# Decoder layer on one core: the first three products of the up stage's first unit, run inside the mix stage

## The reference

```python
h = rmsnorm(x, norm_mix_pre);  proj = h @ w_in
pool_out = multiscale_pool(u_pool, w_pool)          # trailing means, 4 groups of 128
attn_out = stick_breaking_attention(q, k, v)        # 8 heads of 64
merged = concat(rms_normalize(pool_out) * pool_scale, rms_normalize(attn_out) * attn_scale)
mix = merged @ w_out                                # 1024 x 1024
x = x + rmsnorm(mix, norm_mix_post)
h = rmsnorm(x, norm_ffn_pre)
up = causal_depthwise_conv(h @ w_up, conv_w, conv_b)   # 1024 -> 2 x 2816, taps over 3 tokens
gate, val = up[..., :D_FF], up[..., D_FF:]
x = x + rmsnorm((silu(gate) * val) @ w_down, norm_ffn_post)
```

## Time and profile before

| | us |
|---|---|
| median of 3 runs | 2437.66 |
| lowest, highest | 2435.57, 2438.76 |
| the profiled execution's own time | 2436.97 |
| its span | 2435.3 |
| PE busy | 2331.2 (96% of the span) |
| DVE busy | 1817.9 (75%) |
| ACT busy | 1220.9 (50%) |
| POOL busy | 1026.2 (42%) |

### The profile page before, as it was taken

How to read it: one execution, slowest core, us unless ns; L and a number is a source line. 1 busy time by engine, 2 the same in 40 slices (tenths; PEclk the granted TensorE clock), 3 DMA queues, 4 the chain that set the end, 5 groups by cost and what they waited for, 6 DMA issues and landing times. The chain is left out here.

```text
span 2435.3 us, 36769 instructions
## 1 busy us (share of the span) xinstructions
PE 2331.2 (96%) x11673; PEld 1948.4 (80%) x11673; DVE 1817.9 (75%) x2137; ACT 1220.9 (50%) x2101; POOL 1026.2 (42%) x750
## 2 busy tenths in 40 slices
PE   8999999989999999996999999899999999999997
PEld 6787887878888888884888888688888878888876
DVE  5434224999999977878898899999999973344687
ACT  4311114889898975555444444544444433332444
POOL 0000002776666654656455554455455420122653
PEclk9999999999999999997999999999999999999999
DMA  6412347153333225676333233533333225445574
GB/s 192 145 42 89 128 135 193 32 147 92 85 92 87 81 82 173 211 243 214 103 113 103 90 108 102 204 96 108 103 112 103 90 106 174 170 168 203 200 254 160
DMA packets 264699, 324.71 MB, mean 133 GB/s; under 512 B 12996, under 2 KB 185980, under 8 KB 259580
## 3 DMA queue, kind: packets, MB, share of 16 engines
q1 hardware_dynamic: 262268, 314.72, 41.7%
q0 software_dynamic: 2304, 8.39, 0.9%
HBM read 213.48 MB, written 109.58 MB: 133 GB/s over the span
## 5 line engine op out<-in xcount | busy, mean ns | idle before, releaser
L810 POOL TENSOR_TENSOR weight<-beta,stick 128x512 f32<-128x512 f32 (+3 forms) x320 | 304.6, 960 | 539.7 <-ACT beta L749 422.2
L2151 DVE SCALAR_TENSOR_TENSOR x<-up_cols,taps,x 128x1024 f32<-128x1024 f32 x174 | 264.1, 1518 | 14.5 <-ACT x L2048 11.4
L861 DVE TENSOR_TENSOR_SCAN stick<-z_ps,stick,beta 128x512 f32<-128x512 f32 x192 | 245.0, 1276 | 13.2 <-ACT z_ps L750 12.0
L535 PE MATMUL out_ps<-hT,w_hi 128*128 128x512 f32 x768 | 239.6, 393 | 2.4 <-DVEq L462 2.4
L2138 DVE TENSOR_TENSOR wu_lo<-wu_sums,wu_hi 128x512 fp32r<-128x512 f32 x175 | 211.7, 1210 | 0.0
L749 ACT ACTIVATE beta<-z_ps 128x512 f32<-128x512 f32 (+3 forms) x320 | 171.4, 536 | 56.7 <-PE z_ps L893 49.8
L2035 ACT ACTIVATE wu_hi<-wu_sums 128x512 fp32r<-128x512 f32 x175 | 109.5, 627 | 164.0 <-PE gate_odd_ps L2281 90.7
L2281 PE MATMUL value_chain_ps<-wide,wu_hi 128*128 128x512 f32 x528 | 177.3, 390 | 1.9 <-DVE up_cols L2173 1.9
L910 PE MATMUL wT_ps<-ident,weight 128*128 128x128 f32 x1088 | 173.2, 275 | 3.1 <-POOL weight L810 3.1
L535 PEld LDWEIGHTS out_ps<-hT,w_hi 128*128 128x128 f32 x768 | 144.9, 189 | 34.6 <-DVEq L462 2.8
L750 ACT ACTIVATE z_ps<-z_ps 128x512 f32<-128x512 f32 (+3 forms) x320 | 172.2, 538 | 0.0
(11 more groups left out here) (272 smaller groups left out, 6184.7 us busy)
## 6 DMA issues: line engine op xcount, KB each, us to landing
wu_f<-in_w_up SPq DMA_DIRECT2D x44, 512.0 KB, 5.1
bridge<-in_w_up SPq DMA_DIRECT2D x44, 512.0 KB, 5.0
f_scratch<-f_sum SPq DMA_DIRECT2D x88, 256.0 KB, 2.0
down_lo<-f_scratch SPq DMA_DIRECT2D x44, 512.0 KB, 3.4
f_scratch<-x SPq DMA_DIRECT2D x66, 256.0 KB, 2.1
down_b<-in_w_down SPq DMA_DIRECT2D x65, 256.0 KB, 3.9
x_scratch<-x SPq DMA_DIRECT2D x56, 256.0 KB, 2.8
first_head<-qk_scratch SPq DMA_DIRECT2D x24, 512.0 KB, 9.8
```

Source lines behind the costliest of these rows:

```text
L535: m = pe.matmul(out_ps[half + j][:, :], w[slot][:, k, :], hT[h][:, k, j * BANK:(j + 1) * BANK], start=(k == 0 and t == 0), stop=(k == kc - ...
L810: pool.tensor_tensor(weight[v % weight_ring][:, 0:w], beta[v % stick_in][:, 0:w], stick[q % 2][:, at:at + w], ALU.mult).then_inc(weight_do ...
L861: dve.tensor_tensor_scan(stick[q % 2][:, at:at + w][:, ::-1], backwards, beta[u % stick_in][:, 0:w], start, ALU.mult, ALU.bypass).then_inc ...
L2151: dve.scalar_tensor_tensor(out=conv[h], in0=cols[:, h, 2 - back:2 - back + span], scalar=column(kind, h, e), in1=conv[h], op0=ALU.mult, op ...
```

## The change

Operands 0, 1 and 2 and the left operands a11, s1 and a12 are split within the steps of tiles 13 to 15 of mix, into tiles of their own. In PE's step 16, behind the last tile's attention product, stand three products of the up stage's unit 0: a11 with operand 0, s1 with operand 1, and (between the turn of tile 14 and the turn of tile 15) a12 with operand 2. ACT copies the first one's bank to `q` within mix. s2 and operands 3 and 4 (its high half) are also split or loaded at the end of mix. For this the weight block's load moves from step 12 to step 10, the loads of operands 0 and 1 from steps 13 and 14 to 11 and 12, operand 2's to step 15 ahead of the last product, operand 5's from up to the end of mix; POOL's `start_sums` moves from its end to the front of its step 12. SP no longer waits at the end of mix for the loads. The up stage begins with s2; DVE takes `keep_v`, operand 5 and `gate_part` first in unit 0. Scratch tiles change places so that the new ones fit.

```diff
@@ -1060,27 +1068,30 @@
                     if is_tile(t) and not (isinstance(t, int) and t < 2):
                         load_x(t, slot)
                     if isinstance(t, int) and t == tiles - 1:
+
+                        sp.wait_ge(mix_mm_done, done(t - 1))
+                        load_operand(2)
                         sp.wait_ge(mix_mm_done, done(t))
-                        for operand in range(2, 5):
-                            load_operand(operand)
+                        load_operand(3)
+                        load_operand(4)
                     if is_tile(t - 2):
                         store_x(t - 2, slot, uses - 1)
-                    if isinstance(t, int) and t == tiles - 4:
+                    if isinstance(t, int) and t == tiles:
+                        load_operand(5)
+                    if isinstance(t, int) and t == tiles - 6:
 
                         sp.wait_ge(even_out, stored(tiles // 4, 32))
                         sp.wait_ge(b22_out, stored(tiles // 4))
                         sp.wait_ge(sums_out, stored(tiles // 4, 64))
                         for h in range(2):
                             sp.dma_start(up_start["w_f"][:, h, :, :], w_up[0][:, h, :, :]).then_inc(start_w_in, 16)
-                    if isinstance(t, int) and tiles - 3 <= t < tiles - 1:
-                        load_operand(t - (tiles - 3))
+                    if isinstance(t, int) and tiles - 5 <= t < tiles - 3:
+                        load_operand(t - (tiles - 5))
 
                 def load_operand(operand):
-                    sp.dma_start(as_f32(up_start["x_lo"][operand]), s["x7"][operand][:, :, 0:BANK]).then_inc(start_x_in[operand], 16)
-
-                steps(sp, step, after_loop=4)
-                for operand in range(5):
-                    sp.wait_ge(start_x_in[operand], 16)
+                    sp.dma_start(as_f32(up_start["x_lo"][operand]), s["x7"][operand][:, :, 0:BANK]).then_inc(x7_in[operand], 16)
+
+                steps(sp, step, after_loop=6)
@@ -1103,6 +1114,8 @@
                     total(3, t4, b21, t2, ALU.subtract)
 
                 def step(t, slot, uses):
+                    if isinstance(t, int) and t == tiles - 4:
+                        start_sums()
                     if is_tile(t - 2) and slot == 1 and not (isinstance(t, int) and t == tiles + 1):
                         pool.wait_ge(copied, done(t - 2))
                         x_sums(uses - 1)
@@ -1130,8 +1143,7 @@
                     pool.tensor_tensor(s4, a12, s2, ALU.subtract).then_inc(start_sums_done, 1)
                     pool.tensor_tensor(s3, a11, a21, ALU.subtract).then_inc(start_sums_done, 1)
 
-                steps(pool, step)
-                start_sums()
+                steps(pool, step, after_loop=4)
@@ -1157,6 +1169,10 @@
                     act.activation(m_hi[slot][:, :, :], merged_of(t, slot), ACT.Copy).then_inc(m_hi_done, 1)
 
                 def step(t, slot, uses):
+                    if isinstance(t, int) and t == tiles - 1:
+                        act.wait_ge(m_lo_done, done(t))
+                        right_half(1)
+                        left_half(2, "a12")
...
@@ -1183,30 +1199,40 @@
                         else:
                             act.wait_ge(b22_out, stored(uses - 1))
...
+                    if isinstance(t, int) and t == tiles - 1:
+                        act.wait_ge(m_sum, done(t))
+                        right_half(2)
...
+                    if isinstance(t, int) and t == tiles - 3:
+                        right_half(0)
+                    if isinstance(t, int) and t == tiles - 2:
+                        left_half(0, "a11")
+                        left_half(1, "s1")
                     if isinstance(t, int) and t == tiles - 1:
-                        right_half(0)
-                        left_half(0, up_start["w_f"][:, 0, 0:kc // 2, :])
+
+                        act.wait_ge(product_done, 1)
+                        act.activation(up_start["q"][:, :], up_start["gate_even"][:, :], ACT.Copy).then_inc(q_done, 1)
+                        act.wait_ge(mix_mm_done, done(t))
+                        right_half(3)
                     if isinstance(t, int) and t == tiles:
-                        act.wait_ge(mix_mm_done, done(tiles - 1))
-                        right_half(1)
+                        left_half(3, "s2")
+                steps(act, step, after_loop=4)
+                right_half(4)
...
-                        right_low(0, 1)
+                        right_low(2)
                     if is_tile(t + 1):
                         prepare(t + 1, 1 - slot)
+                    if isinstance(t, int) and t == tiles - 2:
+                        right_low(0)
+                    if isinstance(t, int) and t == tiles - 1:
+                        right_low(1)
+                        left_low(2, "a12")
+                        mix_halves(t, slot)
...
+                    if is_tile(t) and not (isinstance(t, int) and t == tiles - 1):
+                        mix_halves(t, slot)
+                    if isinstance(t, int) and t == tiles - 2:
+                        left_low(0, "a11")
+                        left_low(1, "s1")
+                def mix_halves(t, slot):
+                    dve.wait_ge(pool_scaled, done(t))
+                    dve.wait_ge(mix_mm_done, done(t))
+                    dve.scalar_tensor_tensor(out=mix[slot][:, :], in0=attn_ps[:, :], scalar=stat[:, slot, 3:4], in1=mix[slot][:, :],
+                                             op0=ALU.mult, op1=ALU.add).then_inc(mix_done, 1)
+
+                def right_low(operand):
+                    dve.wait_ge(right_half_done, operand + 1)
...
                 steps(dve, step)
-                left_low(0, up_start["w_f"][:, 0, 0:kc // 2, :], 2)
-                right_low(1, 3)
-                left_low(1, up_start["sums"][:, 0, :, :], 4)
+                left_low(3, "s2")
+                right_low(3)
@@ -1319,12 +1357,29 @@
                                                start=(k == 0 and j == 0), stop=(k == n_pool - 1 and j == 2))
...
+                def up_product(bank, i, ready, adds=False):
+                    pe.wait_ge(start_done, ready)
+                    for k in range(kc // 2):
...
+                    m.then_inc(product_done, 1)
+
                 def step(t, slot, uses):
+                    if isinstance(t, int) and t == tiles:
+
+                        pe.wait_ge(pool_scaled, done(tiles - 1))
+                        up_product(up_start["gate_even"], 0, 3)
+                        pe.wait_ge(mix_done, done(tiles - 1))
+                        up_product(up_start["value_last"], 1, 4)
                     if is_tile(t):
                         pe.wait_ge(m_lo_done, done(t))
                         part_product(0, t, slot)
                     if is_tile(t - 2):
                         turn(t - 2, slot)
+                    if isinstance(t, int) and t == tiles:
+                        pe.wait_ge(q_done, 1)
+                        up_product(up_start["gate_even"], 2, 6, adds=True)
                     if is_tile(t):
                         part_product(1, t, slot)
                     if is_tile(t + 1):
...
-                left_half(0, 0, "a12", 0)
-                right_half(0, 2)
-                left_half(0, 0, "s2", 0)
-                keep_q(0, 0)
-                right_half(0, 3)
                 left_half(0, 0, "s4", 0)
...
+                    if first:
+                        keep_v(u, e)
+                        right_low(part, 5)
+                        gate_part(u, e)
...
-                        if first:
-                            right_low(part, 4)
-                            keep_v(u, e)
-                        else:
...
                         if first:
-                            right_low(part, 5)
+                            right_low(part, 6)
+                            copy_taps(0, 0)
+                            copy_taps(1, 1)
...
-                copy_taps(0, 0)
-                left_low(0, 0, "a12")
-                right_low(0, 2)
-                left_low(0, 0, "s2")
-                right_low(0, 3)
+                right_low(0, 4)
                 left_low(0, 0, "s4")
...
-                        pe.wait_ge(v_done, u - 1)
-                    product(value_last[e], 1, 1)
-                    ready(u, "a12", part)
-                    pe.wait_ge(q_done, u + 1)
-                    product(gate_even[e], 2, 2, adds=True)
+                    if not is_first(u):
+                        ready(u, "s1", part)
+                        if not begins:
+                            pe.wait_ge(v_done, u - 1)
+                        product(value_last[e], 1, 1)
+                        ready(u, "a12", part)
...
                     product(value_chain[e], 6, 6, adds=True)
 
-                opening(0, 0, 0)
```

134 lines of the change are left out of this document (68 added, 66 removed).

## The result

Seven runs of the changed kernel took 2444.51 us in the median (2444.39 to 2449.77), seven of the kernel before beside them 2435.57 (2433.89 to 2438.76): a ratio of 1.0039, 95% interval 1.0029 to 1.005. It is slower, by 8.9 us, where I had forecast 2436.9 and at most 2442.5. The forecast counted from the 2437.66 that the kernel before took in its first three runs; as a difference it was 0.8 us faster.

A forecast was written before the change was run, and what follows sets the result against it. The mix-to-up border was taken as bound by a DVE, POOL and ACT relay, then DVE's list. 9.9 us less DVE work against 9.1 us later up gave 0.8 us faster, 2436.9; own range 2433 to 2441.5, overall 2430 to 2442.5.

The forecast's parts named there:

- a12's restart and the tail: End of mix: a12 runs 4.8 us at low clock before tile 15's turn; up starts 9.1 us later than before.
- The stall at tile 15: Mix: tile 15's low half comes 6.0 us later, PE stalls 4.5 us, plus 0.8 for the low-clock restart.
- Loads: nothing waits on them closely: Mix: weights and operands 0 and 1 requested two steps earlier behind the same stores, at no cost.
- The delay of tile 12: Mix: POOL's weight sums, 7.0 us from 1066.3, make tile 12's addition 4.6 us late; ends 2.9 and 8.0.
- POOL holds the tiles up: Rival, mix: sums ahead of tile 12's addition delay it 8.0 us; 5.7 us slower, 2443.4; chance 0.14.
- DVE then needs 29.89 less 9.9, that is 20.0: Up, unit 0: DVE's microseconds from the barrier to the end of the addition freeing a22, a 9.9 us credit.
- A load decides in up: Rival, up: operand 6's load holds ACT's high half, DVE waits 2.2 us; 2439.1; chance 0.10.
- Buffers: Places of tiles in SBUF: named as a possible meaning of differences over a microsecond behind unit 0 or ahead of tile 11.

The follow-up runs named there:

- e1: Changed kernel with only GpSimd's four weight sums moved behind tile 13's addition and store: 2441.09 us, ratio 1.0026.
- e10: Changed kernel with, at tile 15, operand 2's high half behind the mix's square and root and a12's low half behind the mix: 2441.48 us, ratio 1.0032.
- e9: Changed kernel with VectorE's gate_odd and value_odd additions in up's unit 0 ahead of the taps and unit 1's low halves: 2442.86 us, ratio 1.0021.
- e8: Changed kernel with only operand 6 loaded behind operand 5 within mix instead of in up: 2445.81 us, ratio 1.0037.
- e4: Kernel before with a 512-byte pad ahead of attention's second mixed buffer, mix's statistics moved clear of it: 2437.1 us, ratio 1.001.
- e16: Changed kernel with only the 512-byte pad ahead of attention's second mixed buffer taken out: 2444.25 us, ratio 1.004.
- e17: e12 with operand 0's high half later on ScalarE, weight sums ahead of the wait for tile 13's store, and no 512-byte pad: 2436.34 us, ratio 0.9996.
- e12: Changed kernel with later sums and operand loads, a12 behind the turn, value_odd earlier, e10's order, weights' load in two halves: 2434.71 us, ratio 1.0.

## Why the prediction was wrong

**a12's restart and the tail: right. The stall at tile 15: there, in part by luck.** PE waits at tile 15 for VectorE, 2.72 us where 4.5 was forecast, and loses 4.7 us there with the low clock, where 5.3 was forecast. But the low half of tile 15 was 11.3 us late and not 6.0 (it ended at 1101.03, less 3.3); the wait stayed short only because PE itself, held at tile 14, came 6.7 us late. In the tail a12 runs at the low clock in 4.60 us (4.8), tile 15's mix ends 3.9 us behind the last attention product (3.8), its hn 12.0 us behind that (12.2), and up starts 23.7 us behind the last product (24.8).

**"Loads: nothing waits on them closely": wrong.** This is the step that failed in mix. I looked at who waits for the moved loads, and not at what waits behind them in SyncE's queue and beside them in the DMA engines. The earlier trace rows had GpSimd's wait for tile 10's store at 2.69 us, and at 5.07 us for tile 12's, the next that it shows, which stood behind the weights' load in the kernel before. With the weights two tiles earlier the wait for tile 10's store became 4.99 us; with operand 0 early that for tile 11's was 7.74, and tile 14's rows came 3.02 us late. The loss at tile 14, 6.1 us, was nowhere in my sum. The landings over all the runs show what each load delays; how much of the time each is worth stays open, since neither moved alone changes it.

**The delay of tile 12: mis-sized.** The sums took 7.3 us where 7.0 was taken. Their start was 7.0 us later than taken. Of this 3.3 is the store's issue, most of it tile 10's longer wait (2.30), and 3.7 the landing. Not all of the landing is the loads' doing: I had taken 4.6 us from issue to landing, and in the trace of the kernel before this very store took 5.8, hidden in GpSimd's idle time, so 1.2 us of it was mis-sized before anything moved. In the changed kernel it took 8.0. Tile 12 is 11.9 us late, far beyond the 7 from which "POOL holds the tiles up" decides. That rival had the right sign, and in time (2443.4) it comes near, but partly by luck: it forecast 5.7 us of loss and 8.9 were measured, and it put all of the stall at tile 15 and none at tile 14. e1 gives the sums' own share as some 3.4 us of time, with intervals that overlap.

**"DVE then needs 29.89 less 9.9, that is 20.0": wrong.** It needed 23.3. This is the step that failed in up. I took 10.06 us of instructions out of VectorE's list and left the rest at their durations in the kernel before, where GpSimd ran beside that rest for less than half of the time:

```profile
1131.10:1151.00 19.90, 14.54 (x50) 10.91 (x48) 19.90 (x18) 9.32 (x11) 9.18 (x7) 0.83 0.44 130
```

In the changed kernel GpSimd's first work behind the barrier stands beside the rest: it was busy 20.86 of the 23.4 us from up's start (window above). On balance the forms that stayed grew by the 3.3 us: the low half of a11 for unit 1 from 0.68 us to 1.50, and the two taps copies took 1.30 where I took 0.15 for the one added. The Trainium skill says in its GPSIMD Engine Reference, section Specifications, that GpSimd and VectorE share interfaces to SBUF. I quoted that and said that it changed nothing. This trace agrees with it, and so does e10's tail; by this trace it is worth up to 3.3 us, though no run moved GpSimd's work in up alone. Behind it a22 started after 6.9 us of idle time and took 5.46 us where it took some 3: 2.4 us more that I hadn't priced, though the earlier trace rows had the price of a restart. e9 shows that VectorE's list sets when a22 starts: with the addition earlier the wait falls to 1.60 us and the slow product goes.

**"A load decides in up": wrong**, by e8. The wait of 6.20 us for it is real and is off the path.

**Buffers.** The differences ahead of mix and in down nearly cancel (3.3 and -4.2). I had named the places of tiles as what they might mean. In e4 the pad alone, without the change, came with both (mix 6.1 us later, down 3.5 us shorter), so they needn't belong to the moved products; e16 and e17 don't settle it.

## What to carry to other kernels

When work is moved into a busy stage, price its transfers first: ask which stores and loads share the queue and the DMA engines in that stretch, and which engine stands still until such a store has landed. Instructions taken out of one engine's list don't leave at their old durations if another engine's work closes up beside what stays. And a wait of TensorE cost up to as much again here in the products behind it (2.93 us of waits at tile 14 and 2.7 at the low clock), so a wait is priced with its restart.

## What the hardware did that I had not expected

- Waits of 2.9 us in two parts (1.83 and 1.10, tile 14) were followed by a product at a granted clock of 0.64, 2.7 us longer than at full speed. Waits of 1.25 us (e1, tile 15) and 2.00 us (e12, tile 15) weren't: the 5.6 us behind each had a granted clock of 1.00.
- The same VectorE addition of 128x1024 values (tile 14's scaling) took 2.31 us beside GpSimd's weight sums, and 1.22 without them (e1, 1080.02 us), though GpSimd's addition of tile 12 ran beside it from 1080.19. In the kernel before it also took 2.31 us beside GpSimd's block sums (1080.55), so it is not the weight sums alone.
- A wait of 6.2 us of ScalarE for a load, taken away whole (e8), changed no time that could be told.
